# Splitting the first two output tiles of a product at the last two of their inputs

## The reference, cut to what matters

```
def conv_ffn(h, w_up, conv_w, conv_b, w_down):        # called as x + conv_ffn(rms_norm(x, norm_ch[i]), ...)
    u = h @ w_up
    up = jnp.pad(u, ((0, 0), (pad, pad), (0, 0)))
    acc = up[:, :s] * conv_w[0] + conv_b
    for t in range(1, CONV_WIDTH):
        acc = acc + up[:, t:t + s] * conv_w[t]
    gate, val = jnp.split(acc, 2, axis=-1)
    return (jax.nn.silu(gate) * val) @ w_down
```

## Time and profile before

| what | value |
|---|---|
| median of 3 runs | 3680.17 us (3674.91 to 3681.12) |
| the profiled execution's own time | 3677.95 us |
| its span | 3676.2 us |
| PE busy | 3396.6 us, 92% of the span |
| PE weight loads | 2714.2 us, 74% |
| DVE, ACT, POOL busy | 2032.4, 1457.4, 724.5 us (55%, 40%, 20%) |
| mean granted TensorE clock | 0.957 |

### The profile page before, as it was taken

The page is one execution under the profiler, slowest core; times in us unless marked ns, Lnnn a source line. Parts: engine busy times, 40 slices in busy tenths (PEclk is TensorE's granted clock), DMA queues, the critical chain, the costliest instruction groups (busy, mean ns, idle before and its releaser), DMA issues. The chain is left out here.

```text
span 3676.2 us, 46527 instructions
## 1 busy us (share of the span) xinstructions
PE 3396.6 (92%) x18696; PEld 2714.2 (74%) x18696; DVE 2032.4 (55%) x2976; ACT 1457.4 (40%) x2402; POOL 724.5 (20%) x496
## 2 busy tenths in 40 slices
PE   8988999999878999988899997978999999989998
PEld 6656788878557888866687875757888888768787
DVE  6665534355564534465556465536666666546454
ACT  6435322344354222334543233444444444334232
POOL 1000302120002202110011012315444444201010
PEclk9989999999889999998999998999999999989999
DMA  4101322222003222210122222541000000022222
GB/s 147 35 1 60 103 96 97 93 80 81 1 9 100 98 94 95 97 57 1 53 97 101 84 96 82 175 159 38 21 24 24 24 24 33 7 86 98 92 92 80
DMA packets 82292, 260.48 MB, mean 71 GB/s; under 512 B 9632, under 2 KB 13216, under 8 KB 81696
## 3 DMA queue, kind: packets, MB, share of 16 engines
q1 hardware_dynamic: 71424, 236.02, 19.1%
q10 hardware_dynamic: 10656, 21.50, 1.6%
HBM read 236.51 MB, written 20.97 MB: 70 GB/s over the span
## 5 line engine op out<-in xcount | busy, mean ns | idle before, releaser
L1580 DVE TENSOR_TENSOR mlp_w_lo<-mlp_ring,mlp_w_hi 128x1024 fp32r<-128x1024 f32 (+1 forms) x211 | 252.2, 1196 | 602.9 <-ACT mlp_w_hi L1560 602.5
L1560 ACT ACTIVATE mlp_w_hi<-mlp_ring 128x1024 fp32r<-128x1024 f32 (+1 forms) x211 | 213.2, 1011 | 702.7 <-PE ps L1538 696.4
L1580 DVE TENSOR_TENSOR ffn_w_lo<-ffn_ring,ffn_w_hi 128x1024 fp32r<-128x1024 f32 (+3 forms) x172 | 222.6, 1294 | 471.1 <-ACT ffn_w_hi L1560 471.1
L1560 ACT ACTIVATE ffn_w_hi<-ffn_ring 128x1024 fp32r<-128x1024 f32 (+3 forms) x172 | 187.3, 1089 | 511.1 <-PE ps L1538 506.3
L1537 PE MATMUL ps<-mlp_more_parts,mlp_w_hi 128*128 128x512 f32 x952 | 375.5, 394 | 0.0
L1536 PE MATMUL ps<-mlp_more_parts,mlp_w_hi 128*128 128x512 f32 x760 | 309.3, 407 | 43.0 <-DVE mlp_w_lo L1580 24.3
L1536 PE MATMUL ps<-tiles_parts,mlp_w_hi 128*128 128x512 f32 x832 | 331.2, 398 | 5.7 <-issue 5.7
L1536 PE MATMUL ps<-ffn_x_parts,ffn_w_hi 128*128 128x512 f32 x792 | 312.1, 394 | 22.7 <-DVE ffn_x_parts L2290 21.0
L1538 PE MATMUL ps<-tiles_parts,mlp_w_lo 128*128 128x512 f32 x832 | 328.9, 395 | 0.0
L1537 PE MATMUL ps<-ffn_x_parts,ffn_w_hi 128*128 128x512 f32 x792 | 309.9, 391 | 0.0
L1538 PE MATMUL ps<-ffn_x_parts,ffn_w_lo 128*128 128x512 f32 x792 | 309.7, 391 | 0.0
(11 more groups left out here) (489 smaller groups left out, 7018.3 us busy)
## 6 DMA issues: line engine op xcount, KB each, us to landing
ffn_ring<-in_w_ffn_up SPq DMA_DIRECT2D x88, 512.0 KB, 3.2
mlp_ring<-in_w_up SPq DMA_DIRECT2D x64, 512.0 KB, 3.3
mlp_ring<-in_w_down SPq DMA_DIRECT2D x64, 512.0 KB, 3.2
rwkv_keep<-ffn_ring ACTq DMA_DIRECT2D x64, 256.0 KB, 2.3
sq<-rwkv_keep SPq DMA_DIRECT2D x64, 256.0 KB, 2.8
ffn_ring<-in_w_ffn_down SPq DMA_DIRECT2D x16, 768.0 KB, 4.3
in_ring<-in_w_in SPq DMA_DIRECT2D x22, 512.0 KB, 3.3
mlp_ring<-in_w_in SPq DMA_DIRECT2D x22, 512.0 KB, 3.2
```

Source lines behind the costliest of these rows:

```text
L1560: nc.scalar.activation(w.w_hi[:, n % SPLIT, 0:width], w.ring[:, n % RING, 0:width], ACT.Copy).then_inc(s["w_hi_ready"], 1)
L1580: nc.vector.tensor_tensor(w.w_lo[:, n % SPLIT, 0:width], w.ring[:, n % RING, 0:width], w.w_hi[:, n % SPLIT, 0:width].bitcast(F32), ALU.sub ...
```

## The change

PE takes the slots in another order of work. Where a product has one part, more than four inputs, and the next slot is of the same source of inputs, the first tile takes all but its last two inputs, then the second tile takes all but its last two, then the first its last two, then the second its last two. The second tile goes to its own PSUM bank. `slots_used` of the first tile and what follows a tile (`followed`: sums, rotations, small products) come after its last input, as before. The gates product and `w_in` count as one source (`source=first`). ACT, DVE, POOL and SP keep their programs. The pairs are 25: the gates with the first tile of `w_in` (2), the out products (4), the MLP's two up products in each layer (4), the gate product (2), qkv (1), the FFN's two up products and two down products in each layer (8), and RWKV's r, k, v and g1 (4).

```diff
+LATE = 2
@@ class Linear
+        self.source = source or self
@@ chain, PE's program
+            def products(n, first, last):
+                lin, t, part = slots[n]
                 tile = lin.place[t]
+                if first == 0:
+                    if part == 0 and tile >= banks:
+                        pe.wait_ge(s["bank_free"][tile % banks], tile // banks)
+                    pe.wait_ge(s["w_lo_ready"], n + 1)
                 into = m.ps[:, tile % banks, :]
-                for k in range(lin.ks):
+                for k in range(first, last):
                     if t == 0:
                         lin.arrived(pe, s, part * lin.ks + k)
...
+                if last == lin.ks:
+                    mm.then_inc(s["slots_used"], 1)
+                    followed(lin, t, part)
...
+            n = 0
+            while n < len(slots):
+                lin, t, part = slots[n]
+                early = lin.ks - LATE
+                if lin.parts == 1 and t == 0 and early > LATE and n + 1 < len(slots) and slots[n + 1][0].source is lin.source:
+                    for first, last in ((0, early), (early, lin.ks)):
+                        products(n, first, last)
+                        products(n + 1, first, last)
+                    n += 2
+                else:
+                    products(n, 0, lin.ks)
+                    n += 1
```

More of the change, by code:

```diff
@@ L1437, with __init__ @@
 class Linear:
-    def __init__(self, weights, base, tiles, ks, rhs, arrived, parts=1, after_first=None, on_act=None, on_dve=None, on_pool=None, last=0):
+    def __init__(self, weights, base, tiles, ks, rhs, arrived, parts=1, after_first=None, on_act=None, on_dve=None, on_pool=None, last=0, source=None):
         self.weights, self.base, self.tiles, self.ks, self.parts = weights, base, tiles, ks, parts
         self.rhs, self.arrived, self.after_first = rhs, arrived, after_first
+        self.source = source or self
         self.on_act, self.on_dve, self.on_pool, self.last = on_act, on_dve, on_pool, last
@@ L1523, in _ @@
         def _(pe):
-            for n, (lin, t, part) in enumerate(slots):
+            def products(n, first, last):
+                lin, t, part = slots[n]
                 tile = lin.place[t]
-                if part == 0 and tile >= banks:
-                    pe.wait_ge(s["bank_free"][tile % banks], tile // banks)
-                pe.wait_ge(s["w_lo_ready"], n + 1)
+                if first == 0:
+                    if part == 0 and tile >= banks:
+                        pe.wait_ge(s["bank_free"][tile % banks], tile // banks)
+                    pe.wait_ge(s["w_lo_ready"], n + 1)
                 into = m.ps[:, tile % banks, :]
-                for k in range(lin.ks):
+                for k in range(first, last):
                     if t == 0:
@@ L1535, in _, with followed @@
                     ends = part == lin.parts - 1 and k == lin.ks - 1
[L1536 to L1541, removed]
+                    nc.tensor.matmul(into, w_hi, hi, start=(part == 0 and k == 0), stop=False, skip_group_check=True)
+                    nc.tensor.matmul(into, w_hi, lo, start=False, stop=False, skip_group_check=True)
+                    mm = nc.tensor.matmul(into, w_lo, hi, start=False, stop=ends, skip_group_check=True)
+                if last == lin.ks:
+                    mm.then_inc(s["slots_used"], 1)
+                    followed(lin, t, part)
+            def followed(lin, t, part):
                 if part == lin.parts - 1:
+                    if lin.after_first and t in lin.after_first:
+                        lin.after_first[t](pe, s)
                     for small, u in behind.get((lin, t), ()):
@@ L1919, in in_projection @@
     act, dve = taken(y, vec[:, V1["b_in"]:V1["b_in"] + NIN], "p_biased", False)
-    return [first, Linear(a["w_in"], layer * NIN, NIN, DT, normed.rhs, normed.arrived, 1, {t: beside(t) for t in range(NIN)}, act, dve, last=2)]
+    return [first, Linear(a["w_in"], layer * NIN, NIN, DT, normed.rhs, normed.arrived, 1, {t: beside(t) for t in range(NIN)}, act, dve, last=2, source=first)]
 def qkv_product(nc, m, a, normed, y, prep):
```

## The result

Over 20 runs each the changed kernel took 3690.86 us (3678.61 to 3706.65) and the kernel before 3679.39 (3674.91 to 3684.72): ratio 1.0032, 95% interval 1.0024 to 1.0041, some 12 us slower. The forecast was 3682 us and no change, and the chance that I gave to slower by over 0.2% was 0.23; by the median that is what came, 0.32% slower. The time lies inside the range of 3670 to 3694, but on the side that I held less likely. The profiled execution has a span of 3691.9 us against 3676.2.

The account below looks back on a forecast made before the run. PE, busy 92% of the span, was taken as the bound. Gains of 21.3 and 0.7 us against losses of 13.0 and 10.6 gave +1.6, so 3682 us on the median of 3680.17, forecast as no change; range 3670 to 3694.

Parts of the forecast that it names:

- four downs: FFN down products, both layers: second tile's work fills PE's waits for the last two inputs; 21.3 us gained, between 17 and 23.
- start of the first chain and its gates: First chain: 0.7 us gained at a wait on the second-last input, 2.0 lost at the gates' fourth slot.
- nine plain refills: Four out products, four second up products and r: PE idles 1.27 us and restarts 0.1 slower; 12.3 us lost.
- k, v, g1: RWKV products: small products cover most of the refill behind k and v, 0.2 us lost each; g1 loses 0.3.
- The gain: Down products gain 21.3 us, with 1.4 taken off for the clock in the second ones; first chain's start gains 0.7.
- Loss 1: Pairs with nothing between the tiles: only 1.36 us hide the third slot's refill of 2.63; 13.0 us lost, between 9 and 18.
- Nothing: the second slot's weights are there 2.6 us after the start: All pairs: second slot's weights are needed 1.36 us earlier but come before the first six inputs' 4.08 us end; no cost.
- Loss 2: Nine pairs with a norm's sums between: root, reciprocal and scaling come late for gates, FFN up and qkv; 10.6 us lost.
- Theory B: Posed in the follow-ups: the changed program slows the untouched mixers and RWKV heads for good, by some 10 us; no chance given.
- The clock falls at every refill: Rival, slower: idle of 1.3 to 2.3 us at 13 refills drops PE's clock, 25 us, 3705 us; chance 0.10 with lesser forms.
- A late ACT and DVE stay late: Rival, slower: RWKV's and the in products' later slots stall too, 8 us more in 8 pairs, 3690 us; chance 0.13.
- The chain is hidden: Rival, faster: gates' and qkv's root and reciprocal don't reach PE, 9.9 us fall away, 3672 us; chance 0.17.

Follow-up runs that it names:

- e5: The changed kernel once more with no edit, against the kernel before: 3689.8 us, ratio 1.0023.
- e2: New order only in the four FFN down products, two inputs held back, against the kernel before: 3655.65 us, ratio 0.9931.
- e4: New order only in the twelve 8-input pairs with no sums between and no late input, against the kernel before: 3705.3 us, ratio 1.0064.
- e6: Changed kernel with all 25 pairs but three inputs held back instead of two, against the kernel before: 3673.95 us, ratio 0.9982.
- e7: Changed kernel with all pairs but four inputs held back instead of two, against the kernel before: 3665.16 us, ratio 0.9954.
- e1: The kernel before, unchanged, run and profiled once more against the same program: 3675.48 us against 3682.9, ratio 0.9985.
- e10: New order only in the nine norm pairs, with DVE's reciprocal replaced by a short scaling (value left out); one profiled execution, 3678.86 us.
- e11: Control: the kernel before, old order, with DVE's reciprocal replaced by the same short scaling; one profiled execution, 3666.53 us.
- e3: New order only in the nine pairs with a norm's sums between the tiles, against the kernel before: 3702.6 us, ratio 1.0060.

## Why the prediction was right or wrong

Its own terms, forecast and then the profile after (the products of e5 agree to 0.3 us):

| term | forecast | measured |
|---|---|---|
| four downs | −21.3 | −18.7 |
| start of the first chain and its gates | −0.7 + 2.0 | +1.4 |
| second gates | +2.0 | +2.8 |
| nine plain refills | +12.3 | +11.4 |
| k, v, g1 | +0.7 | +2.0 |
| FFN first up products | +0.7 | 0.0 |
| MLP first up products | 0 | −3.0 |
| qkv | +5.9 | +8.3 |
| sum of the products (with smaller ones) | +1.6 | +4.5 |

- *The gain.* The order of events was right: third tiles came 18.65 us after the start as worked out (18.6). What was mis-sized is the clock: I counted its fall for the second downs (1.4), where idle of 1.44 and 1.66 us left it at 1.00, and not for the first downs, where an idle of 2.16 cost 1.6 us each. e2 shows that the same idle can leave it alone. Another 0.9 us that the second down product of layer 0 had gained by its third tile (6.5) was gone when r began, in PE's wait for RWKV's inputs, which the sum had not looked at.
- *Loss 1.* 1.16 us of wait and 0.08 of restart against 1.27 and 0.1. Shown by the steps of e4, e6 and e7. Against e1, whose first and last out products were 1.5 and 0.7 us shorter than in the first profile, the 11.4 us are 13.9, so this term is known to some 2.5 us. The step "Nothing: the second slot's weights are there 2.6 us after the start" failed for k: its first tile stands behind the one-tile product w1, and ACT had other work ahead of the second slot's weights. ACT and DVE around k's start after (start, us, line, idle before):
```profile
2339.53 1.30 ACT L2308 ACTIVATE ffn_hid<-ffn_acc 128x512 fp32r<-128x512 f32 x2 [3.38 <-DVE ffn_acc L2302]
...
2340.74 1.04 ACT L1582 ACTIVATE ffn_w_hi<-ffn_ring 128x1024 fp32r<-128x1024 f32 x1
...
2341.81 2.06 DVE L1602 TENSOR_TENSOR ffn_w_lo<-ffn_ring,ffn_w_hi 128x1024 fp32r<-128x1024 f32 x1 [1.65 <-ACT ffn_w_hi L1582]
```
  k began at 2338.34; DVE's subtraction, 2.06 us beside POOL's work where it is 1.23 alone, ended at 2343.87, 5.5 us later and not 2.6. The row for it stood in the trace before (the subtraction ran from 2323.66 to 2325.73 for a product that began at 2321.64, 4.1 us), and I had checked the second slot only where nothing else ran.
- *Loss 2.* The wait at L850 was forecast at about 4 and is 4.21. Behind it the clock ran at its lower level, 1.2 GHz, for 4.7 us (0.50):
```profile
1617.00:1619.90 2.90, 0.01 (x1) 0.01 (x1) 2.87 (x3) 2.15 (x5) 0.00 (x0) 0.81 0.18 72
1619.90:1624.60 4.70, 4.70 (x9) 3.08 (x10) 3.62 (x5) 0.60 (x1) 0.00 (x0) 0.50 0.32 112
```
  That cost 2.2 us, 2.0 forecast. The 2.4 above the forecast are two falls of the clock later in qkv (1.6 us each, at tiles 7 and 9, one of them made good before the product's end): the first behind a wait of 2.37 us at L861 that was there before and had left the clock at 1.00, the second behind small matmuls without a wait. That the chain is the cause of the wait is shown by e10 and e11. The gates' fourth slot waited 1.72 and 1.81, forecast 1.9.
- *MLP up products.* −1.5 each are no work of the order: e3 has +0.1 and 0.0 there with the new one, e4 −1.2 and +1.35 with the old one. Behind the wait of 2.85 us at the start of the first of them the clock was 0.81 and 0.50 in two stretches of 2 us before, and 1.00 after and in e4: the clock's phase, not the order.
- *The rest.* The measured 12 us (8.5 in e5's session) are more than the 4.5 in the products. The profile has the rest in stages that do the same work at a lower granted clock; over the eleven other profiles that part lay between −4.1 and +17.6, for the old order at 6.1 and −0.3. Whether the change makes such a draw likelier is open: the three profiles of the old order (mean 1.9) and two of the new (9.0) are too few. Theory B in the form of a fixed 10 us is out, since e2, the new program with 21 of its 25 pairs switched off, has +2.6, and e6 and e7, with all pairs, −4.1 and −2.9. A weaker form is not: both profiles of the changed kernel have the two mixer stages at 163.5 and 166.8 us (first profile before 159.5 and 164.8, e1 164.4 and 164.2), and by the ratios (times 3680, less the products) 7 us lie outside the products in the change and 4 in its repeat, 6 and 7 in e3 and e4, −0.6 in e2 and −3 in the unchanged kernel. So 5 to 7 of the measured 12 us, by which profile of before one takes, have no shown cause.
- *Rivals.* "The clock falls at every refill" is out; a lesser form of it came true at the two 12-input refills. "A late ACT and DVE stay late" came true in r alone, where each tile from the third to the last fell behind by 0.19 us more, 1 us in all. "The chain is hidden" is out. The Trainium skill, "TensorE: Matmul & The Clock Gate", section "A second HAM failure mode: psum-queue depth-cycling", tells of short idles between groups of matmuls that cycle through PSUM banks, by which the clock keeps changing level. The first downs after agree with that; the same downs in e2 and the 8-input refills don't: it was worth 3.3 us here, where the rival's sum was 25.

The sum hit a gap of two nearly equal numbers, 22 us gained and 24 lost. Each was right within 3, and the sign of the difference was never better known than that.

## What to carry to other kernels

Holding back the last inputs of a tile covers a late input only where one is late; everywhere else it takes cover away from the refill of a double-buffered operand: count what then runs between the release of a buffer and its next use (1.36 us here against a refill of 2.6), and hold back enough work to hide it. Apply such an order by place, with the trace's list of late inputs in hand: the same edit made the kernel 0.7% faster in four products and 0.6% slower in each of two other groups, some 0.4 to 0.7% of it in the products themselves. And follow the first tile's result, not only its buffer: a chain that ended half a microsecond before PE needed it became a wait of 4.2 us when its start moved by 4.

## What the runs showed of the hardware

- Behind an idle of PE of 2.16 us after full work the granted clock was lower in both layers of the changed kernel, in both of its profiles (0.51 to 0.59 in the 3.4 us behind), and 1.00 in both layers of e2. Behind the second downs' 1.66 us the matmuls kept 0.39 us each in both layers, behind the 4.21 us in qkv the clock was 0.50.
- Stages in which PE often waits for DVE for a short time vary between executions of the same code with the granted clock: the stretch of the first mixer stage had 159.9 us at 0.85 and 167.9 at 0.80. The interval of a ratio of two sets of runs of the same program left 1 out, by 0.03%.
- DVE's reciprocal of 128x512 took 3.35 us, a scaling of the same size 0.43. Its subtraction of 128x1024 took 1.23 us alone and up to 2.06 us in r and k, where POOL worked beside it.
